# Decode attention with an output projection spread thinner, a ring of four value places, and an earlier sample merge

## The reference, cut to what matters

```python
def block(s, qb):
    ...
    s1 = jnp.einsum('bqhd,bkhd->bhqk', q1b, k1).astype(jnp.float32) * scale + bias
    s2 = jnp.einsum('bqhd,bkhd->bhqk', q2b, k2).astype(jnp.float32) * scale + bias
    a = masked_softmax(s1, mask) - lam * masked_softmax(s2, mask)
    return jnp.einsum('bhqk,bkhd->bqhd', a.astype(v.dtype), v)
...
o = jax.nn.sigmoid(ga) * o_a + jax.nn.sigmoid(gb) * o_b
h = x + jnp.einsum('bte,ed->btd', o, w_o)
hn = rmsnorm(h, mlp_g)
y = h + jnp.einsum('btf,fd->btd', jnp.square(jax.nn.relu(jnp.einsum('btd,df->btf', hn, w_up))), w_down)
```

## Time and profile before

| what | value |
|---|---|
| time, median of 3 runs (lowest, highest) | 1647.08 us (1645.26, 1650.61) |
| the profiled execution | 1650.32 us, span 1648.6 us |
| granted TensorE clock, mean over the span | 0.959 |
| TensorE busy, products | 1528.9 us (93%) |
| VectorE, ScalarE, GpSimd busy | 834.8, 596.4, 193.8 us |
| moved by transfers | 276.27 MB, mean 168 GB/s |

### The profile page before, as it was taken

How to read it: one execution, slowest core, us unless ns; L and a number is a source line. 1 busy time by engine, 2 the same in 40 slices (tenths; PEclk the granted TensorE clock), 3 DMA queues, 4 the chain that set the end, 5 groups by cost and what they waited for, 6 DMA issues and landing times. The chain is left out here.

```text
span 1648.6 us, 31808 instructions
## 1 busy us (share of the span) xinstructions
PE 1528.9 (93%) x12584; PEld 1257.7 (76%) x12584; DVE 834.8 (51%) x1812; ACT 596.4 (36%) x1162; POOL 193.8 (12%) x287
## 2 busy tenths in 40 slices
PE   7999999999999999989887999498968999999998
PEld 5888888878899957656555555366648999999998
DVE  4866623216998588867752232254544432234322
ACT  5332211325555377667642121133333331133210
POOL 1010000001443000844210000000000000000000
PEclk9999999999999989998988999699978999999999
DMA  7634478434343473335237865899864343434321
GB/s 207 200 118 168 169 267 289 155 92 101 102 126 102 121 215 95 128 112 150 78 113 269 287 241 181 288 362 346 304 236 158 102 127 102 127 102 127 103 76 55
DMA packets 189482, 276.27 MB, mean 168 GB/s; under 512 B 36781, under 2 KB 118125, under 8 KB 189238
## 3 DMA queue, kind: packets, MB, share of 16 engines
q1 hardware_dynamic: 172834, 223.08, 41.8%
q0 software_dynamic: 8352, 33.73, 6.5%
q10 hardware_dynamic: 8180, 17.91, 3.0%
HBM read 249.50 MB, written 44.69 MB: 178 GB/s over the span
## 5 line engine op out<-in xcount | busy, mean ns | idle before, releaser
L799 PE MATMUL pj_ps<-all_hi,pj_xh 128*128 128x512 f32 x480 | 192.0, 400 | 0.4 <-DVE all_lo L671 0.4
L801 PE MATMUL pj_ps<-all_hi,pj_xl 128*128 128x512 f32 x480 | 189.8, 396 | 0.0
L800 PE MATMUL pj_ps<-all_lo,pj_xh 128*128 128x512 f32 x480 | 189.8, 395 | 0.0
L2815 DVE COPY de_slot<-de_ps_t 128x512 f32<-128x512 f32 (+5 forms) x117 | 69.6, 602 | 199.5 <-PE de_ps_t L2483 128.3
L2700 ACT ACTIVATE de_slot<-de_ps_t 128x512 f32<-128x512 f32 (+3 forms) x123 | 63.1, 517 | 265.1 <-PE de_ps_t L2483 147.7
L3284 PE MATMUL fi_ps<-fi_th,fi_wh 128*128 128x272 f32 x512 | 150.0, 293 | 3.3 <-DVE fi_tl L3099 3.3
L3286 PE MATMUL fi_ps<-fi_th,fi_wl 128*128 128x272 f32 x512 | 150.3, 294 | 0.0
L3285 PE MATMUL fi_ps<-fi_tl,fi_wh 128*128 128x272 f32 x512 | 149.4, 292 | 0.0
L3285 PE MATMUL fi_ps<-fi_fl,fi_wh 128*128 128x272 f32 x512 | 148.5, 290 | 0.0
L3284 PE MATMUL fi_ps<-fi_fh,fi_wh 128*128 128x272 f32 x512 | 147.8, 289 | 0.0
L3286 PE MATMUL fi_ps<-fi_fh,fi_wl 128*128 128x272 f32 x512 | 147.7, 288 | 0.0
(11 more groups left out here) (415 smaller groups left out, 3286.4 us busy)
## 6 DMA issues: line engine op xcount, KB each, us to landing
de_dv<-in_cache_diff SPq DMA_DIRECT2D x64, 512.0 KB, 9.0
all_big<-in_w_in SPq DMA_DIRECT2D x14, 2048.0 KB, 10.5
de_dk<-in_cache_diff SPq DMA_DIRECT2D x48, 512.0 KB, 9.7
all_big<-in_cache_nsa SPq DMA_DIRECT2D x64, 256.0 KB, 6.9
all_big<-in_w_up SPq DMA_DIRECT2D x16, 1024.0 KB, 6.1
all_big<-in_w_down SPq DMA_DIRECT2D x16, 1024.0 KB, 5.6
all_dk<-in_cache_diff SPq DMA_DIRECT2D x16, 512.0 KB, 6.6
all_win<-in_cache_win SPq DMA_DIRECT2D x32, 256.0 KB, 8.8
```

Of the source, the lines that this page charges most:

```text
L799: pe.matmul(ps[:, t, :], xh[:, k, xk], wh[:, u, k, :], start=k == 0, stop=False)
L800: pe.matmul(ps[:, t, :], xh[:, k, xk], wl[:, u, k, :], start=False, stop=False)
L801: return pe.matmul(ps[:, t, :], xl[:, k, xk], wh[:, u, k, :], start=False, stop=k == KT - 1)
L2815: ins = nc.vector.tensor_copy(slot[rows, g % 4, cols], ps_t[rows, g % 3, cols])
```

## The change

In decode the projection's parts become one product each, so that a result takes eight double steps, and the pause is six. Every pair from 0 to 2 goes round the four lower value places; only pair 3's pages 4 to 7 use the upper ones, behind the projection's last product. `p_dif` 1 of every pair but the last stands behind the next pair's key page 1, as pair 0's did. The queue has one order for pairs 0 to 2: value pages 0 to 3, key pages 4 and 5, and so on, and pages 4 to 7 ahead of the next pair's key page 2.

In the closing stage both gates and the first mixer's rows are loaded before the last difference is stored, and only that one after it. The first product of the merge is one instruction for both halves, early on VectorE; the second product and the sum follow there too, behind tile 3's low parts, and GpSimd has no part in it. The second half of tokens of the first unit is split in two: tokens 272 to 511 (240 columns) ahead of the merged rows' turn and ahead of their projection, and the 32 sample tokens behind the last turn. Copying the merged rows moves ahead of the second weights' split, on ScalarE and VectorE.

```diff
@@ decode_steps
         if i:
-            out += [(i - 1, *x) for x in (DIFF_STEPS[:2] if i == 1 else DIFF_STEPS)]
+            out += [(i - 1, *x) for x in DIFF_STEPS[:2]]
...
-        if i == 1:
-            out += [(0, *x) for x in DIFF_STEPS[2:]]
+        if i:
+            out += [(i - 1, *x) for x in DIFF_STEPS[2:]]
...
-SIDE_FIRST, SIDE_PARTS, SIDE_PAUSE = 5, KT // 2, 5
+SIDE_FIRST, SIDE_PARTS, SIDE_PAUSE = 5, KT, 6
@@ value_place, load_v
-            if i == 0:
-                return k % RING_PAGES, 32 * (k // RING_PAGES + 1)
-            return k, 32 * (i + 2) if k < RING_PAGES else 32 * i
+            if i + 1 == PAIRS and k >= RING_PAGES:
+                return k, 32
+            return k % RING_PAGES, 32 * (2 * i + k // RING_PAGES + 1)
...
-                if i == 1 and k >= RING_PAGES:
+                if i + 1 == PAIRS and k >= RING_PAGES:
                     sp.wait_ge(proj_mm, SIDE_ROWS)
-                elif i == 0 and k >= RING_PAGES:
-                    sp.wait_ge(dv_read, k - RING_PAGES + 1)
-                elif i == 1:
-                    sp.wait_ge(dv_read, RING_PAGES + k + 1)
-                elif i:
-                    sp.wait_ge(dv_read, N_PAGES * (i - 1) + k + 1)
+                elif N_PAGES * i + k >= RING_PAGES:
+                    sp.wait_ge(dv_read, N_PAGES * i + k - RING_PAGES + 1)
@@ the queue, pairs 0 to 2
-                if i == 0:
-                    for k in range(RING_PAGES):
-                        load_v(pages, i, k)
-                    for k in (4, 5):
-                        load_k(pages, i, k)
-                elif i == 1:
-                    for k in (4, 5):
-                        load_k(pages, i, k)
-                    for k in range(N_PAGES):
-                        load_v(pages, i, k)
-                else:
-                    for k in range(6):
-                        load_v(pages, i, k)
-                    load_k(pages, i, 4)
-                    load_v(pages, i, 6)
-                    load_k(pages, i, 5)
-                    load_v(pages, i, 7)
+                for k in range(RING_PAGES):
+                    load_v(pages, i, k)
+                for k in (4, 5):
+                    load_k(pages, i, k)
...
-                    if i == 0 and k == KEYS_FIRST:
+                    if k == KEYS_FIRST:
@@ project_rows
-                for k in (2 * part, 2 * part + 1):
-                    ins = pe.matmul(ps_w[:], o_t[:, k, tile_of(n)], half_wo[:, k, :], start=k == 0, stop=k == KT - 1)
+                ins = pe.matmul(ps_w[:], o_t[:, part, tile_of(n)], half_wo[:, part, :], start=part == 0, stop=part == KT - 1)
@@ finish, SyncE
+            for k in range(2):
+                for j, name in enumerate(("ga", "oa", "gb")):
+                    sp.dma_start(more[k][:, j, :], d[name][SEQ:TOKENS, CW * k:CW * (k + 1)]).then_inc(sample_in[0], 16)
             sp.wait_ge(last_out, 1)
...
-                for j, name in enumerate(("ga", "oa", "gb", "ob")):
-                    sp.dma_start(more[k][:, j, :], d[name][SEQ:TOKENS, CW * k:CW * (k + 1)]).then_inc(sample_in[k], 16)
+                sp.dma_start(more[k][:, 3, :], d["ob"][SEQ:TOKENS, CW * k:CW * (k + 1)]).then_inc(sample_in[1], 16)
@@ finish, GpSimd
-            for k in range(2):
-                b = more[k]
-                pool.wait_ge(sample_in[k], 64)
-                nc.gpsimd.tensor_tensor(b[:, 2, :], b[:, 2, :], b[:, 3, :], ALU.mult).then_inc(second_part, 1)
@@ finish, VectorE
+            def first_samples():
+                dve.wait_ge(sample_in[0], 96)
+                step(nc.vector.tensor_tensor(gated[:, 0, :], gated[:, 0, :], gated[:, 1, :], ALU.mult))
+
+            def merge_samples():
+                dve.wait_ge(sample_in[1], 32)
+                step(nc.vector.tensor_tensor(gated[:, 2, :], gated[:, 2, :], gated[:, 3, :], ALU.mult))
+                nc.vector.tensor_tensor(gated[:, 0, :], gated[:, 0, :], gated[:, 2, :], ALU.add).then_inc(merged, 1)
...
             low_parts("h", 0)
+            first_samples()
             normalize(2)
...
             normalize(3)
-            for k in range(2):
-                merge_samples(k)
             low_parts("h", 3)
+            merge_samples()
+            samples_copied()
             split(1)
-            samples_copied()
@@ finish, TensorE
-            def up(u, f, b):
+            halves = [slice(PAIR * b, PAIR * (b + 1)) for b in range(2)]
+
+            def up(u, f, b, tok=None):
+                tok = tok or halves[b]
+                out = ps[:, 2 * f + b, tok.start - PAIR * b:tok.stop - PAIR * b]
...
             up(0, 1, 0)
+            pe.wait_ge(t_lo, TURN["h", 3, 1] + 1)
+            up(0, 0, 1, slice(PAIR, SEQ))
             turn("o", QT)
+            up(0, 1, 1, slice(PAIR, SEQ))
             project_samples()
             turn("h", QT)
             pe.wait_ge(t_lo, len(TURNS))
-            up(0, 0, 1).then_inc(up_done, 1)
-            up(0, 1, 1).then_inc(up_done, 1)
+            for f in range(2):
+                up(0, f, 1, slice(SEQ, TOKENS)).then_inc(up_done, 1)
```

More of the change, by code:

```diff
@@ L90 @@
     "down_done", "h_added", "h_sq", "h_root", "relued", "f_hi", "f_lo", "y_added", "f_made0", "f_made1", "y_turned",
-    "y_ready", "y_out", "window_kept", "last_sq", "last_root", "last_out", "last_stored", "dve_step", "zeroed",
-    "second_part")
+    "y_ready", "y_out", "window_kept", "last_sq", "last_root", "last_out", "last_stored", "dve_step", "zeroed")
 class Space:
@@ L2955, in finish @@
         last_sq, last_root, last_out, last_stored = (s.sem(n) for n in ("last_sq", "last_root", "last_out", "last_stored"))
-        step_sem, zeroed, second_part = (s.sem(n) for n in ("dve_step", "zeroed", "second_part"))
+        step_sem, zeroed = (s.sem(n) for n in ("dve_step", "zeroed"))
         block = ctx.enter_context(nc.Block())
@@ L3067, in _ @@
             high_parts("h", 3)
+            copy_samples()
             split(1)
-            copy_samples()
             root(QT)
@@ L3155, in split @@
                 nc.vector.tensor_tensor(wl[:, n, :], w[:, n, :], wh[:, n, :].bitcast(F32), ALU.subtract).then_inc(w_split, 1)
-            def merge_samples(k):
-                b = more[k]
-                dve.wait_ge(sample_in[k], 64)
-                step(nc.vector.tensor_tensor(b[:, 0, :], b[:, 0, :], b[:, 1, :], ALU.mult))
-                dve.wait_ge(second_part, k + 1)
-                nc.vector.tensor_tensor(b[:, 0, :], b[:, 0, :], b[:, 2, :], ALU.add).then_inc(merged, 1)
+            def first_samples():
[5 more added lines that the diff above has]
+                nc.vector.tensor_tensor(gated[:, 0, :], gated[:, 0, :], gated[:, 2, :], ALU.add).then_inc(merged, 1)
             nc.vector.memset(eps[:], EPS).then_inc(zeroed, 1)
@@ L3262, in turn @@
                     else:
-                        pe.wait_ge(merged, k + 1)
+                        pe.wait_ge(merged, 1)
                         src = more[k][:, 0, :]
@@ L3280, in project_samples, with product @@
                 ins.then_inc(o_done, 1)
-            def product(o, k, n_k, b, hi, lo, a_hi, a_lo):
-                tok = slice(PAIR * b, PAIR * (b + 1))
+            def product(o, k, n_k, tok, hi, lo, a_hi, a_lo):
                 pe.matmul(o, hi[:, k, :], a_hi[:, k, tok], start=k == 0, stop=False)
@@ L3291, in up @@
                 for k in range(KT):
-                    ins = product(ps[:, 2 * f + b, 0:PAIR], k, KT, b, hi, lo, th, tl)
+                    ins = product(out, k, KT, tok, hi, lo, th, tl)
                 return ins
@@ L3308, in down_products @@
                     for b in range(2):
-                        ins = product(ps[:, 4 + 2 * u + b, 0:PAIR], k, FT, b, hi, lo, fh, fl)
+                        ins = product(ps[:, 4 + 2 * u + b, 0:PAIR], k, FT, halves[b], hi, lo, fh, fl)
                 return ins
```

## The result

The changed kernel takes 1654.3 us (median of 20 runs, 1647.7 to 1661.4), the kernel before 1646.6 (20 runs): ratio 1.0048, interval 1.0037 to 1.006, so 7.9 us slower, 6.1 to 9.9. The forecast was 1656.

What follows compares the result with a forecast made beforehand. TensorE sets the pace, waiting for key pages in decode. Decode 0 (31.5 us of waits go, 31.5 come) plus closing stage +9.4 on 1650.3 gives 1659.7; the median lies 3.2 below the profiled run, so 1656, range 1641 to 1667.

Steps and rivals of the forecast that it cites:

- The long wait of pair 1: Decode, TensorE at key page 6 of pair 1: the 19.8 us wait goes, some 4 us stay.
- Pair 3, page 4: Decode: this key page lands 18.8 us after the difference product starts, wanted at 7.6, a new wait of 11.2 us.
- The 2.5 for page 6: Decode, pair 3: key page 6 lands 9.0 us after page 4, for 2.5 us more of wait.
- Pair 1: Decode: late key pages 4 to 7 of pair 1, w_o's load taking its share; 14 us of new waits, bounds 7 and 18.
- the third rival: Decode, w_o's second half lands 15 us after issue; projection row 4 and pair 1's pages 4 to 6 wait: 1664, chance 15%.
- Pair 2 and page 2 of pair 3: Decode, new key-page waits: 2.5 us (0 to 5) in pair 2, 1 us (0 to 2) at pair 3's page 2.
- Decode's sum: Decode: new waits of 31.5 us against 31.5 that go, so unchanged, with bounds of -10 and +10.
- The closing stage: Split products, merge and projection after decode: +9.4 us in sum, bounds +2.2 and +11.
- The small products: Closing stage, TensorE: 48 products of 32 columns at the low clock, 0.21 us each, 10.2 us.
- The six small loads: Closing stage, SyncE's queue: moved ahead of the last difference's store, which waits for VectorE in any case, at 0 cost.
- The clock: Closing stage: TensorE stays at the low clock through the 32-column products; the next unit's first 24 products cost 2.4 us more.
- the first two cases: Closing stage: clock stays low, 1650 to 1662, 45%; or comes back within the 32-column products, +4.7, 1652, 20%.

## Why the prediction came out

**The long wait of pair 1**: gone, as said; what blocked SyncE's queue was the order, and 2.73 us of the 19.8 stay (forecast some 4).

**Pair 3, page 4**: forecast 11.2, measured 11.23, and the page's turn came 18.87 us after the product (forecast 18.8). The line that was put together from one burst held for another. The 2.5 for page 6 behind it did not come.

**Pair 1**: this term was mis-sized: 14 forecast, 4.14 + 1.49 + 2.73 + 0.32 = 8.7 measured. Page 4 was 4.14 late and not 5.5, pages 5 and 7 hardly, and the price of w_o lay at its own row and not at the keys. The collision that the third rival spoke of was there, but a page's wait ahead of it covered it: w_o took 18.2 us to land, against 9.2. Those 9.2 were not quite "alone", as the prediction has it: SyncE's next value burst was issued from 968.4 on, 5.4 us after that load.

**Pair 2 and page 2 of pair 3**: 1.98 and nothing, forecast 2.5 and 1.

**Decode's sum**: 0 forecast, -2.8 between the two profiles, -1.2 (-4.0 to +1.8) in the run of decode alone. That it came out is in part luck. The new waits were forecast at 31.5 and measured 21.9. But the forecast charged 5 us of low clock to the waits that go, and to those that come next to none. Decode before and after, in the columns of the stretches above:

```profile
852.12:1211.38 359.26, 309.97 (x3713) 207.80 (x3713) 128.56 (x358) 88.29 (x172) 19.87 (x36) 0.92 0.79 280
847.57:1204.04 356.47, 314.41 (x3712) 209.15 (x3713) 129.29 (x360) 88.10 (x170) 19.97 (x36) 0.92 0.78 283
```

TensorE stood idle for 7.2 us less, and was busy for 4.4 more with the same products. In pairs 1 to 3, read in stretches of a quarter of a microsecond, it worked some 19.5 us at 0.50, before 10.8; at half the clock about half of that is lost, an estimate of 10 us against 5. So the waits were put some 10 us too high and the clock behind them some 10 too low.

**The closing stage**: +9.4 forecast, +9.4 in the profiles, 8 in the run of the stage alone. The small products: 48 x 0.213 = 10.26 (forecast 10.2), and 26 low products behind them (forecast 24). The 240 columns: 0.112 each (forecast 0.116). Two terms were off and cancelled. The way from decode's last group to the first 272-column product grew by 1.2 us, 22.6 to 23.75, and not by 0.3. Some 1.0 of it lies ahead of the first turn, where the first norm on VectorE waits longer for its gain (a small load on SyncE's queue); before, after, and after's first product of the sample rows:

```profile
1221.59 1.41 DVE L3144 SCALAR_TENSOR_TENSOR fi_norm_rows<-all_big,fi_rstd,fi_gain 128x512 f32<-128x512 f32 x2 [0.79 <-DMA fi_gain<-in_mlp_norm]
1215.27 1.42 DVE L3122 SCALAR_TENSOR_TENSOR fi_norm_rows<-all_big,fi_rstd,fi_gain 128x512 f32<-128x512 f32 x2 [1.74 <-DMA fi_gain<-in_mlp_norm]
1220.72 0.68 DVE L3137 TENSOR_TENSOR fi_gated<-fi_gated 64x512 f32<-64x512 f32 x1 [0.68 <-DMA fi_gated<-scratch_gb]
```

The six small loads, which the prediction put at 0, now follow right behind the gain's load on that queue. In the two profiles with the old order that wait is 0.8, in the eleven with the new one 0.7 to 4.8; that the six loads make it longer is likely but not shown. The third turn came another 0.7 later, since the first product of the sample rows on VectorE waited 0.68 for its load and stands ahead of that turn's norm; most of this came back at the next wait (2.05 against 2.62). In return the clock rose after 13 of the first 24 products, before only after all of them, some 1.1 us. Merge and turn of the sample rows were waited for by nobody, as said, so that bringing them forward gained nothing by itself.

**The clock**, on which the first two cases parted: nothing came back within the small products. The Trainium skill, TensorE: Matmul & The Clock Gate, Part 1, says that the warm-up is a budget of time in which TensorE is busy, and not a number of products. The runs do not agree for products of 32 columns: busy 10.10 of 10.10 us at 0.50, and in the run with the projection first a fall from 1.00 to 0.50 with TensorE busy throughout. For 272 columns no run tells time from number, since all these products go at one pace: the rise came after 12 of them (2.9 us) in the run with all 272 columns, and after 24 (5.5 us) in the kernel before.

What stays open: the single gains by ratios are 4 to 5 us larger or smaller than the profiles' stages say (the projection first: 5.6 against 9.4; the 272 columns: 7 against 2; the projection as before: 3.8 against none); the time at which decode begins moves by 7 us between executions, and the wait for the gain by 4, and each profile is one execution.

## What to carry to other kernels

Put a load into a queue by when its data is wanted, not by when its place is free: value pages wanted 40 us later cost 11 us at a key page wanted now. When a wait goes, look at once for what it had been covering. Work that is ready belongs behind the start of a chain on other engines, not ahead of it; and a product cut down to a few columns is not cheap: at the full clock 32 columns took 0.11 us, as 240 did, each with a load of weights of its own, and the clock may fall.

## What the runs showed of the hardware that I had not expected

Forty-eight products of 32 columns took 10.3 us, and of 272 columns, at the same place behind the same idle time, 7.4. A dense stream of 32-column products brought the granted clock from 1.00 to 0.50 behind 37 of them, with no idle time within the stream, where 272-column products at the same place held it at 1.00; the earlier trace rows had hinted at it. One load of 2 MB on ScalarE's queue took 18.2 us to land beside SyncE's bursts (issued at 994.9 in the changed kernel), 18.5 with the values last (issued at 995.9, behind pages of the selected branch), 11.6 when issued 1.6 us ahead of such pages, and 9.2 in the earlier trace rows.
